# Queries and keys projected together in units of one k block and 1024 columns

## The chip, the cores and the metric

The kernel runs on one core of one Trainium2 chip. The metric is the device time of one execution in microseconds; the time before is the median of three runs. The core's engines are TensorE (PE in the profile, its weight loads PEld), VectorE (DVE), ScalarE (ACT), GpSimd (POOL) and SyncE (SP), which issues most of the transfers.

## The reference

One decoder layer on x of 256 tokens x 1024 features, in float32. A combined projection gives the columns of a retention part and of a block attention part; both outputs are concatenated and go through one output projection, then a SwiGLU network follows.

```python
h = rmsnorm(x, pre_mix_norm)
proj = h @ w_in                                  # 1024 x 3072
rq, rk, rv, rg, mq, mk, mv = split(proj)         # 256, 256, 512, 512, 512, 512, 512 columns
ret = silu(rg) * head_rmsnorm(retention(rotary(rq), rotary(rk) * 64 ** -0.5, rv))
moba = moba_attention(mq, mk, mv, rel_bias)      # 8 heads of 64, causal softmax in one block of 256
x = x + rmsnorm(concat([ret, moba]) @ w_out, post_mix_norm)
h = rmsnorm(x, pre_ffn_norm)
x = x + rmsnorm((silu(h @ w_gate) * (h @ w_up)) @ w_down, post_ffn_norm)
```

## The kernel before

**Arithmetic.** Each float32 operand of a projection is split into a rounded high part and a rest, both in a format that TensorE takes at one pass. ScalarE makes the high part (`w_hi`, `a_hi`), VectorE the rest (`w_lo`, `a_lo`). A product of a 128x128 tile of x and 128x512 of weights is then three matmuls into one PSUM bank (`product`, L940 to L944): hi by hi, hi by lo, lo by hi. The norm's gain is folded into x; the row factor 1/rms is applied when PSUM is copied out.

**Units.** `w_in` is cut into six groups of 512 columns, in the order attention queries (0), attention keys (1), attention values (2), retention queries and keys (3), retention values (4), retention gate (5). A group is four units; a unit is 128x1024 of weights (512 KB): two k blocks of 128 rows, 512 columns of each. There are 24 units, u = 0 to 23, and TensorE does 12 matmuls in each: 2 token tiles, 2 k blocks, 3 products. Group g accumulates over its four units in the two banks of `pj[g % 2]`, one bank for each token tile: bank01 for even groups, bank23 for odd ones. So the copies out of one group run while TensorE fills the other pair.

**Transfers.** SyncE issues all weights in one queue, in the order of units (L343 to L371). `raw` has six slots: the load of unit n waits for `lo_ready` n - 5. The first four units (HALVED) are loaded in two halves of 512 columns, with the transposed x between them: block 0 alone (with the gains), block 1 alone, then pairs of blocks, one pair per unit. x in natural layout (`xs`, for the row factors) goes out ahead of units 5 and 6. GpSimd issues the relative bias: a small row is computed by TensorE after unit 1 (L1021), copied by ScalarE (`brow`), stored, and read back as a 1 MB tile (L425), for which it also waits until all eight `x_lo` are there.

**ScalarE and VectorE.** Before the main loop ScalarE goes through units 0 to 3 (L472 to L486): half of the weights, one block of x, the other half, the next block; then `hi_in(4)`. In step u of the main loop it does `hi_in(u + 5)` (LEAD), which waits for the transfer and for a free slot of the ring of eight, and around it what the attention needs. The placement is by hand: the brow copy in step 0, squares of x in steps 0 and 1 (L527), the query copies `rows_out(qn, ...)` in step 4 after `hi_in(9)`, their transposed copies in step Q_T + 1 = 7 (L517), the key copies in step 8 after `hi_in(13)`, their transposed copies in step K_T + 1 = 10. VectorE mirrors this with `lo_in`.

**TensorE.** In units 0 to 3 `first_unit` (L962) waits for each half by itself. From unit 4 on one wait for `lo_ready` covers the unit. Before a group reuses a pair of banks, TensorE waits for the copies out of them: group 2 for `q_nat` (L996), group 3 for `k_nat`. After unit 6 it transposes the queries (L1023), after unit 9 the keys (L1029), each in eight 128x128 transposes, and from unit 10 on it does the scores of one head after each unit.

`wait_projection` (L303) tells who copies when a group's tile is complete: tile 0 by `proj_done`, tile 1 by `w_used` after the fourth unit of the group.

Of the kernel before, what the change touches and what calls it, by code (L numbers as in the profile page):

```python
# [15 lines left out]
P = 128  # L34
D = 1024
S = 256
# [16 lines left out]
UPG = NK * CW // UNIT  # L53
KPU = UNIT // CW
N_IN = NG * UPG
WOUT_K = [4, 5, 6, 7, 0, 1, 2, 3]
# [17 lines left out]

Q_T, K_T, S0, RQK_T = 6, 9, 10, 18
PT_LAG, PV_LAG = 2, 3
# [12 lines left out]
def hybrid_layer(nc, xt, x, g_post_mix, g_pre_ffn, g_post_ffn, rel_bias,  # L89
                 w_in, w_out, w_gu, w_dn, ident_c, rope_c, decay_c, bucket_c, bias_row, out):  # L90
    with ExitStack() as ctx:
# [101 lines left out]
        d_used = sem("d_used")  # L193
        xt_loaded = [sem(f"xt_loaded{i}") for i in range(NK // KPU)]
        xt_first = sem("xt_first")
        x_loaded = [sem(f"x_loaded{t}") for t in range(NT)]
# [90 lines left out]
        def wait_x_block(eng, k):  # L287

            if k == 0:
                eng.wait_ge(xt_first, 16)  # L290
            elif k == 1 or k % KPU == 0:
                eng.wait_ge(xt_loaded[k // KPU], 16)

# [9 lines left out]
        def wait_projection(eng, group, t):  # L303
            if t == 0:
                eng.wait_ge(proj_done, group + 1)
            else:
                eng.wait_ge(w_used, UPG * (group + 1))
# [23 lines left out]
        def _(sp):  # L331
# [5 lines left out]

            def load_x(k0, k1, done):

                a, b = (NK + k0 * S if k0 else 0), NK + k1 * S  # L340
                sp.dma_start(xT[:, a:b], xt[:, a:b]).then_inc(done, 16)

            for n in range(N_IN):  # L343
                if 5 <= n < 5 + NT:
                    sp.dma_start(xs[:, n - 5, :], x[(n - 5) * P:(n - 4) * P, :]).then_inc(x_loaded[n - 5], 16)
                if n == 6:
                    sp.dma_start(ident[:, :], ident_c).then_inc(ident_loaded, 16)
                if n < HALVED:

                    for i in range(KPU):  # L350
                        sp.dma_start(raw[:, n, i * CW:(i + 1) * CW], w_in[n][:, i * CW:(i + 1) * CW]
                                     ).then_inc(raw_half[n] if i == 0 else raw_loaded[n], 16)
                        if n == 0:
# [96 lines left out]
        def _(act):  # L450
# [20 lines left out]
            act.activation(warm[:, :], half[:, :], ACT.Copy).then_inc(warmed, 1)  # L471
            for i in range(NK // KPU):  # L472
                for k in range(KPU * i, KPU * (i + 1)):
                    if i < HALVED:

                        cols = slice(k % KPU * CW, (k % KPU + 1) * CW)
                        if k % KPU == 0:
                            act.wait_ge(raw_half[i], 16)
                        else:
                            wait_raw(act, i)  # L480
                        act.activation(w_hi[:, i, cols], raw[:, i, cols], ACT.Copy
                                       ).then_inc(hi_half if k % KPU == 0 else hi_ready, 1)
                    wait_x_block(act, k)
                    act.activation(a_hi[:, k, :], x_block(k), ACT.Copy, scale=gain(k)).then_inc(x_hi, 1)
                if i >= HALVED:
                    hi_in(i)  # L486
            hi_in(4)

# [18 lines left out]
            for u in range(N_IN):  # L507
# [152 lines left out]
        def _(dve):  # L660
# [21 lines left out]

            for i in range(NK // KPU):
                for k in range(KPU * i, KPU * (i + 1)):
                    if i < HALVED:
                        cols = slice(k % KPU * CW, (k % KPU + 1) * CW)
                        dve.wait_ge(hi_half if k % KPU == 0 else hi_ready, i + 1)
                        dve.tensor_tensor(w_lo[:, i, cols], raw[:, i, cols], w_hi[:, i, cols].bitcast(F32),
                                          ALU.subtract).then_inc(lo_half if k % KPU == 0 else lo_ready, 1)
                    wait_x_block(dve, k)  # L690
                    dve.wait_ge(x_hi, k + 1)
                    dve.scalar_tensor_tensor(out=a_lo[:, k, :], in0=x_block(k), scalar=gain(k),
                                             in1=a_hi[:, k, :].bitcast(F32), op0=ALU.mult,
                                             op1=ALU.subtract).then_inc(x_lo, 1)
                if i >= HALVED:
                    lo_in(i)
            lo_in(4)

# [33 lines left out]
            for u in range(N_IN):  # L732
# [15 lines left out]
                if u <= S0 + PT_LAG + MH:  # L748
                    for n in LO_UNITS.get(u, [u + LEAD]):
                        lo_in(n)  # L750
                if u < NT:
                    factor(X_, u, 2 * u + 2)
# [186 lines left out]
        def _(pe):  # L939
# [22 lines left out]
            def first_unit(u):  # L962

                for i in range(KPU):
                    k, cols = KPU * u + i, slice(i * CW, (i + 1) * CW)
                    pe.wait_ge(hi_half if i == 0 else hi_ready, u + 1)
                    pe.wait_ge(x_hi, k + 1)
                    for t in range(NT):
                        pe.matmul(pj[0][:, t, :], a_hi[:, k, tile(t)], w_hi[:, u, cols],  # L969
                                  start=(k == 0), stop=False)  # L970
                    pe.wait_ge(lo_half if i == 0 else lo_ready, u + 1)
                    for t in range(NT):
                        pe.matmul(pj[0][:, t, :], a_hi[:, k, tile(t)], w_lo[:, u, cols],  # L973
                                  start=False, stop=False)
                    pe.wait_ge(x_lo, k + 1)
                    for t in range(NT):
                        ins = pe.matmul(pj[0][:, t, :], a_lo[:, k, tile(t)], w_hi[:, u, cols],  # L977
                                        start=False, stop=(k == NK - 1))
                        if t == 0 and k == NK - 1:
                            ins.then_inc(proj_done, 1)  # L980
# [5 lines left out]
            for u in range(N_IN):  # L986
# [3 lines left out]
                else:  # L990
                    pe.wait_ge(lo_ready, u + 1)
                for t in range(0 if u < HALVED else NT):
                    if s == 0:
# [9 lines left out]
                    for i in range(KPU):  # L1003
                        k = KPU * s + i
                        if g == 0 and t == 0:
                            pe.wait_ge(x_lo, k + 1)
                        ins = product(pj[g % 2][:, t, :], a_hi[:, k, tile(t)], a_lo[:, k, tile(t)],
# [3 lines left out]
                    if s == UPG - 1 and t == 0:  # L1011
                        ins.then_inc(proj_done, 1)
                if u >= HALVED:
                    ins.then_inc(w_used, 1)
# [227 lines left out]
def _laid_out(i):  # L1242

    def a(name):
        return np.asarray(i[name])

    x = a("x")[0]
    w_in = a("w_in")[0].reshape(UPG, KPU, P, NG, CW)[:, :, :, ORDER]
    gate = a("w_gate")[0].reshape(GU, KPU, P, NF, FG)
# [8 lines left out]
        "rel_bias": a("rel_bias"),  # L1258
        "w_in": w_in.transpose(3, 0, 2, 1, 4).reshape(N_IN, P, UNIT),
        "w_out": a("w_out")[0].reshape(NK, P, D)[WOUT_K],  # L1260
# [18 lines left out]
```

## Time and profile before

| | us |
|---|---|
| median of 3 runs | 318.85 |
| lowest and highest run | 318.06, 322.44 |
| span of the profiled execution | 316.7 |
| TensorE busy in it | 307.7 (97%) |
| VectorE busy | 180.9 (57%) |
| ScalarE busy | 150.9 (48%) |
| GpSimd busy | 24.6 (8%) |

The profile is of one execution; its span is what the engines' records cover, and the times of the runs hold a little around it too. Busy times of different engines overlap and do not add up. Matmuls are pipelined: the record of one is longer than the distance to the next.

### The profile page before, as it was taken

To read this page: it belongs to the slowest core of one execution; us is meant where nothing else is said; L and a number is where in the kernel's file an instruction comes from. 1 tells how busy PE (TensorE), PEld (TensorE's weight loads), DVE (VectorE), ACT (ScalarE), POOL (GpSimd) and SP (SyncE) were. 2 spreads that over 40 slices of the span, in tenths; PEclk is the share of its full clock that TensorE was granted. 3 is DMA by queue.
4 is the path that set the end of the run, shared out by engine and by line. 5 is a ranking of instruction groups with operands and counts; after the bars stand their busy time and mean duration, and the time that the engine had idled before them with its cause. 6 is when DMAs were issued, how large, how long until landed. Compare 5 with 4: busy or idle time off the path is not lost.

```text
span 316.7 us, 4110 instructions
## 1 busy us (share of the span) xinstructions
PE 307.7 (97%) x1432; PEld 247.1 (78%) x1432; DVE 180.9 (57%) x255; ACT 150.9 (48%) x248; POOL 24.6 (8%) x27
## 2 busy tenths in 40 slices
PE   6999999999999999999999999999999999999992
PEld 3788867778888888778888888888888888888881
DVE  2858447675467497899555555544444454551426
ACT  5887654436409164676444444444433333340322
POOL 2020045000002000540000000000000000000001
PEclk9999999999999999999999999999999999999998
DMA  7999994405451553279955555555655655400003
GB/s 212 405 406 378 411 395 138 148 26 184 150 155 46 199 155 112 71 220 314 340 179 174 179 193 185 167 178 191 199 199 199 199 197 192 141 0 0 0 2 132
DMA packets 17518, 58.35 MB, mean 184 GB/s; under 512 B 1998, under 2 KB 2518, under 8 KB 17505
## 3 DMA queue, kind: packets, MB, share of 16 engines
q1 hardware_dynamic: 17136, 57.06, 52.3%
q0 software_dynamic: 368, 1.11, 1.0%
q8 instruction: 8, 0.13, 0.2%
q14 instruction: 6, 0.04, 0.0%
HBM read 57.10 MB, written 1.06 MB: 184 GB/s over the span
## 4 chain that ended last, share of the span: by engine, by line
PE 90%; DVE 4%; POOL 2%; DMA 2%; ACT 1%; issue 0%; SPq 0%; DVEq 0%
PE bank L942 26%; PE bank L944 26%; PE bank L943 25%; PE bank L952 4%; DMA raw<-in_w_in 2%; PE bank L969 1%; POOL xs L442 1%; PE bank L1043 1%; PE bank L1041 1%; PE bank L973 1%; PE bank L977 1%; DVE d_lo L867 1%; DVE res L933 1%; DVE w_lo L860 1%; PE bank L1075 1%; DVE res L927 1%
## 5 line engine op out<-in xcount | busy, mean ns | idle before, releaser
L942 PE MATMUL bank<-w_hi,a_hi 128*128 128x512 f32 x256 | 101.7, 397 | 0.0
L944 PE MATMUL bank<-w_hi,a_lo 128*128 128x512 f32 x256 | 100.1, 391 | 0.0
L943 PE MATMUL bank<-w_lo,a_hi 128*128 128x512 f32 x256 | 99.7, 390 | 0.0
L944 PEld LDWEIGHTS bank<-w_hi,a_lo 128*128 128x128 f32 x256 | 48.0, 188 | 10.5
L942 PEld LDWEIGHTS bank<-w_hi,a_hi 128*128 128x128 f32 x256 | 48.1, 188 | 10.3 <-issue 0.7
L608 ACT ACTIVATE sil<-bank,rstd 128x256 f32<-128x256 f32 x22 | 10.4, 473 | 95.8 <-PE bank L944 93.4
L943 PEld LDWEIGHTS bank<-w_lo,a_hi 128*128 128x128 f32 x256 | 48.1, 188 | 9.8
L860 DVE TENSOR_TENSOR w_lo<-raw,w_hi 128x1024 fp32r<-128x1024 f32 x40 | 49.5, 1276 | 6.5 <-ACT w_hi L593 6.5
L875 DVE SCALAR_TENSOR_TENSOR hid<-bank,rstd,sil 128x256 f32<-128x256 f32 x22 | 10.6, 484 | 74.3 <-ACT sil L608 74.3
L672 DVE TENSOR_TENSOR w_lo<-raw,w_hi 128x1024 fp32r<-128x1024 f32 x32 | 40.3, 1281 | 17.9 <-ACT w_hi L456 17.9
L593 ACT ACTIVATE w_hi<-raw 128x1024 fp32r<-128x1024 f32 x40 | 40.4, 1057 | 0.0
L942 PE MATMUL bank<-d_hi,h_hi 128*128 128x512 f32 x88 | 36.6, 415 | 0.2 <-DVE d_lo L867 0.2
L456 ACT ACTIVATE w_hi<-raw 128x1024 fp32r<-128x1024 f32 x32 | 32.7, 1051 | 6.6 <-DMA raw<-in_w_in 4.3
L944 PE MATMUL bank<-d_hi,h_lo 128*128 128x512 f32 x88 | 34.8, 395 | 0.0
L943 PE MATMUL bank<-d_lo,h_hi 128*128 128x512 f32 x88 | 34.3, 390 | 0.0
L867 DVE TENSOR_TENSOR d_lo<-raw,d_hi 128x1024 fp32r<-128x1024 f32 x22 | 26.0, 1218 | 0.9 <-ACT d_hi L601 0.9
L601 ACT ACTIVATE d_hi<-raw 128x1024 fp32r<-128x1024 f32 x22 | 22.3, 1059 | 0.8 <-DMA raw<-in_w_dn 0.8
L410 POOL TENSOR_TENSOR rstd<-va,half 128x1 f32<-128x1 f32 x8 | 5.3, 669 | 201.7 <-DVE va L678 201.7
L944 PEld LDWEIGHTS bank<-d_hi,h_lo 128*128 128x128 f32 x88 | 16.5, 188 | 3.9
L942 PEld LDWEIGHTS bank<-d_hi,h_hi 128*128 128x128 f32 x88 | 16.5, 188 | 3.4 <-DVE d_lo L867 0.6
L943 PEld LDWEIGHTS bank<-d_lo,h_hi 128*128 128x128 f32 x88 | 16.6, 189 | 2.9
L513 ACT ACTIVATE pr<-pr,lmin 128x128 f32<-128x128 f32 (+1 forms) x16 | 7.2, 448 | 18.7 <-DVE lmin L726 18.7
(116 smaller groups left out, 299.2 us busy)
## 6 DMA issues: line engine op xcount, KB each, us to landing
raw<-in_w_gu SPq DMA_DIRECT2D x44, 512.0 KB, 4.5
raw<-in_w_dn SPq DMA_DIRECT2D x22, 512.0 KB, 4.7
raw<-in_w_in SPq DMA_DIRECT2D x20, 512.0 KB, 9.1
raw<-in_w_out SPq DMA_DIRECT2D x8, 512.0 KB, 3.2
raw<-in_w_in SPq DMA_DIRECT2D x8, 256.0 KB, 5.5
xs<-in_x SPq DMA_DIRECT2D x2, 512.0 KB, 8.2
bias<-bias_row POOLq DMA_DIRECT2D x1, 1024.0 KB, 9.8
out<-res SPq DMA_DIRECT2D x4, 256.0 KB, 2.0
```

The lines of the kernel that those rows point to most:

```text
L456: act.activation(w_hi[:, n % RING, :], raw[:, n % RAW, :], ACT.Copy).then_inc(hi_ready, 1)
L593: act.activation(w_hi[:, a0 % RING, :], raw[:, n0 % RAW, :], ACT.Copy).then_inc(hi_ready, 1)
L601: act.activation(d_hi[:, (DN * g0 + j) % DRING, :], raw[:, n0 % RAW, :], ACT.Copy).then_inc(hi_ready, 1)
L608: act.activation(sil[:, t, :], pg[:, t, 0:FG], ACT.Silu, scale=rstd[:, X1_, t:t + 1]).then_inc(sil_ready[t], 1)
L672: dve.tensor_tensor(w_lo[:, n % RING, :], raw[:, n % RAW, :], w_hi[:, n % RING, :].bitcast(F32), ALU.subtract).then_inc(lo_ready, 1)
L860: dve.tensor_tensor(w_lo[:, slot, :], raw[:, n0 % RAW, :], w_hi[:, slot, :].bitcast(F32), ALU.subtract).then_inc(lo_ready, 1)
L867: dve.tensor_tensor(d_lo[:, slot, :], raw[:, n0 % RAW, :], d_hi[:, slot, :].bitcast(F32), ALU.subtract).then_inc(lo_ready, 1)
L875: dve.scalar_tensor_tensor(out=hid[:, t, :], in0=pg[:, t, FG:2 * FG], scalar=rstd[:, X1_, t:t + 1], in1=sil[:, t, :], op0=ALU.mult, op1=AL ...
L942: pe.matmul(acc, hi, wh, start=first, stop=False)
L943: pe.matmul(acc, hi, wl, start=False, stop=False)
L944: return pe.matmul(acc, lo, wh, start=False, stop=last)
L952: ins = pe.transpose(dst[:, b * P:(b + 1) * P], src[:, b * P:(b + 1) * P], ident[:, :])
```

## The change

Groups 0 and 1 (queries and keys) are taken together as eight units (QK = 8) of one k block and 1024 columns: the left half of a unit is queries, the right half keys. All four banks, `pj[0]` and `pj[1]`, are filled over units 0 to 7. The bytes of a unit, the matmuls of a unit and their number in all stay as they are; groups 2 to 5 are unchanged. With this:

- x is loaded in eight single blocks, block n + 1 behind the weights of unit n; ScalarE and VectorE round block k + 1 behind unit k: blocks 0 to 5 ahead of the main loop, 6 and 7 in its steps 0 and 1, after `hi_in(5)` and `hi_in(6)`.
- `first_unit` uses the same block of x for both halves and writes them to different pairs of banks; a new `both_unit` does units 4 to 7, in the order queries tile 0, queries tile 1, keys tile 0, keys tile 1.
- The query copies move from step 4 of ScalarE's loop to step 7, after `hi_in(12)`; the key copies from step 8 to step 7, right behind them and ahead of `hi_in(13)`.
- The query transposes move from unit 6 to unit 8 (Q_T), their copies from step 7 to step 9. The keys' stay.
- `wait_projection` counts anew, and the host lays `w_in` out accordingly.

```diff
-Q_T, K_T, S0, RQK_T = 6, 9, 10, 18
+Q_T, K_T, S0, RQK_T = 8, 9, 10, 18
...
         def wait_projection(eng, group, t):
-            if t == 0:
-                eng.wait_ge(proj_done, group + 1)
+
+            if (group, t) == (0, 1):
+                eng.wait_ge(proj_done, 2)
+            elif t == 0:
+                eng.wait_ge(proj_done, group + 1 + min(group, 1))
+            elif group == 1:
+                eng.wait_ge(w_used, QK)
             else:
                 eng.wait_ge(w_used, UPG * (group + 1))
...
                     for i in range(KPU):
                         sp.dma_start(raw[:, n, i * CW:(i + 1) * CW], w_in[n][:, i * CW:(i + 1) * CW]
                                      ).then_inc(raw_half[n] if i == 0 else raw_loaded[n], 16)
-                        if n == 0:
-                            load_x(i, i + 1, xt_first if i == 0 else xt_loaded[0])
-                        elif i == 0:
-                            load_x(KPU * n, KPU * (n + 1), xt_loaded[n])
-                elif n < NK // KPU:
-                    load_x(KPU * n, KPU * (n + 1), xt_loaded[n])
+                        if n == 0 and i == 0:
+                            load_x(0)
+                    load_x(n + 1)
+                elif n < NK:
                     load(n, n % RAW, w_in[n])
+                    if n + 1 < NK:
+                        load_x(n + 1)
...
+            for k in range(LEAD):
+                if k < HALVED:
+                    act.wait_ge(raw_half[k], 16)
+                    act.activation(w_hi[:, k, 0:CW], raw[:, k, 0:CW], ACT.Copy).then_inc(hi_half, 1)
+                    if k == 0:
+                        x_hi_part(0)
+                    wait_raw(act, k)
+                    act.activation(w_hi[:, k, CW:UNIT], raw[:, k, CW:UNIT], ACT.Copy).then_inc(hi_ready, 1)
+                else:
+                    hi_in(k)
+                x_hi_part(k + 1)
...
                 hi_in(u + LEAD)
+                if u + LEAD + 1 < NK:
+                    x_hi_part(u + LEAD + 1)
...
-                if u == UPG:
+                if u == QK - 1:
                     act.wait_ge(nq_ready, 1)
                     wait_factor(act, X_, NT - 1)
                     rows_out(qn, 0, lambda t: nq[:, t:t + 1], q_nat)
-                if u == 2 * UPG:
                     rows_out(kn, 1, r_x, k_nat)
...
+            def both_unit(u):
+
+                pe.wait_ge(x_lo, u + 1)
+                for i in range(KPU):
+                    for t in range(NT):
+                        ins = product(pj[i][:, t, :], a_hi[:, u, tile(t)], a_lo[:, u, tile(t)],
+                                      w_hi[:, u, i * CW:(i + 1) * CW], w_lo[:, u, i * CW:(i + 1) * CW],
+                                      first=False, last=(u == QK - 1))
+                        if u == QK - 1 and (i, t) != (KPU - 1, NT - 1):
                             ins.then_inc(proj_done, 1)
                 ins.then_inc(w_used, 1)
```

## Rows read from the trace of the kernel before

**Rows 1.** The page's first part: busy time, share of the span, instructions

```profile
span 316.7 us, 4110 instructions
PE 307.7 (97%) x1432; PEld 247.1 (78%) x1432; DVE 180.9 (57%) x255; ACT 150.9 (48%) x248; POOL 24.6 (8%) x27
```

**Rows 2.** Busy time of each engine in four stretches; last: clock, DMA share, GB/s

```profile
0.00:20.00 20.00, 17.61 (x68) 11.76 (x69) 11.35 (x20) 13.86 (x26) 2.20 (x10) 1.00 0.91 328
20.00:40.00 20.00, 20.00 (x98) 16.28 (x96) 12.35 (x12) 15.14 (x22) 2.07 (x3) 1.00 1.03 396
40.00:60.00 20.00, 20.00 (x97) 15.07 (x97) 11.11 (x28) 10.83 (x27) 8.08 (x3) 1.00 0.65 245
120.00:140.00 20.00, 19.19 (x94) 15.65 (x93) 16.10 (x21) 11.66 (x23) 8.59 (x7) 1.00 0.35 108
```

**Rows 3.** The chain of waits in order of time: start, length, what

```profile
7.13 0.41 ACT a_hi L484
7.67 0.70 PE bank L969 x2
...
26.58 0.87 PE bank L952 x8
...
35.66 0.87 PE bank L952 x8
```

**Rows 4.** Timeline of the first units: start, length, engine, instruction, idle before it

```profile
1.19 0.43 SPq L341 DMA_DIRECT2D xT<-in_xt  x1
4.63 0.51 ACT L484 ACTIVATE a_hi<-xT 128x256 fp32r<-128x256 f32 x1 [0.16 <-DMA xT<-in_xt]
5.28 0.70 PE L969 MATMUL bank<-w_hi,a_hi 128*128 128x512 f32 x2 [0.41 <-ACT a_hi L484]
5.82 0.62 PE L973 MATMUL bank<-w_lo,a_hi 128*128 128x512 f32 x2
6.28 0.61 PE L977 MATMUL bank<-w_hi,a_lo 128*128 128x512 f32 x2
6.50 0.63 ACT L481 ACTIVATE w_hi<-raw 128x512 fp32r<-128x512 f32 x1 [1.36 <-DMA raw<-in_w_in]
7.03 0.49 ACT L484 ACTIVATE a_hi<-xT 128x256 fp32r<-128x256 f32 x1
7.16 0.69 DVE L688 TENSOR_TENSOR w_lo<-raw,w_hi 128x512 fp32r<-128x512 f32 x1 [1.42 <-ACT w_hi L481]
7.47 0.63 ACT L481 ACTIVATE w_hi<-raw 128x512 fp32r<-128x512 f32 x1
7.67 0.70 PE L969 MATMUL bank<-w_hi,a_hi 128*128 128x512 f32 x2 [0.78 <-ACT a_hi L484]
9.12 0.61 PE L969 MATMUL bank<-w_hi,a_hi 128*128 128x512 f32 x2
```

**Rows 5.** Timeline of ScalarE and VectorE around the query copies

```profile
16.86 1.06 ACT L456 ACTIVATE w_hi<-raw 128x1024 fp32r<-128x1024 f32 x1 [1.51 <-DMA raw<-in_w_in]
19.63 1.06 ACT L456 ACTIVATE w_hi<-raw 128x1024 fp32r<-128x1024 f32 x1
20.72 1.23 DVE L672 TENSOR_TENSOR w_lo<-raw,w_hi 128x1024 fp32r<-128x1024 f32 x1 [0.82 <-ACT w_hi L456]
21.96 2.94 ACT L456 ACTIVATE w_hi<-raw 128x1024 fp32r<-128x1024 f32 x3
24.81 1.24 ACT L493 ACTIVATE qn<-bank,nq 128x512 f32<-128x512 f32 x2
27.16 1.06 ACT L456 ACTIVATE w_hi<-raw 128x1024 fp32r<-128x1024 f32 x1 [0.16 <-DMA raw<-in_w_in]
28.12 1.07 ACT L500 ACTIVATE qT<-bank 128x512 f32<-128x512 f32 x2
32.58 1.06 ACT L456 ACTIVATE w_hi<-raw 128x1024 fp32r<-128x1024 f32 x1 [2.44 <-DMA raw<-in_w_in]
```

**Rows 6.** Issues of units 11, 12 and 13, each with its time to landing

```profile
L336 SPq DMA_DIRECT2D raw<-in_w_in x1: 328/328/328, 19.2 to 19.2; - x1
DMA to landing us min/median/max: 7.9/7.9/7.9
...
L336 SPq DMA_DIRECT2D raw<-in_w_in x1: 328/328/328, 22.0 to 22.0; - x1
DMA to landing us min/median/max: 6.5/6.5/6.5
...
L336 SPq DMA_DIRECT2D raw<-in_w_in x1: 327/327/327, 24.3 to 24.3; - x1
DMA to landing us min/median/max: 8.3/8.3/8.3
```

**Rows 7.** Timeline of GpSimd: the bias row stored, the bias tile loaded

```profile
18.57 0.51 POOL L420 DMA_DIRECT2D bias_row<-brow  x1 [15.97 <-ACT brow L523]
23.53 0.96 POOL L425 DMA_DIRECT2D bias<-bias_row  x1 [0.59 <-DMA bias_row<-brow]
```

More of the change, by code:

```diff
@@ L54 @@
 KPU = UNIT // CW
+QK = KPU * UPG
 N_IN = NG * UPG
@@ L193, in hybrid_layer @@
         d_used = sem("d_used")
-        xt_loaded = [sem(f"xt_loaded{i}") for i in range(NK // KPU)]
-        xt_first = sem("xt_first")
+        xt_loaded = [sem(f"xt_loaded{k}") for k in range(NK)]
         x_loaded = [sem(f"x_loaded{t}") for t in range(NT)]
@@ L287, in wait_x_block @@
         def wait_x_block(eng, k):
[L289 to L292, printed above, removed]
+            eng.wait_ge(xt_loaded[k], 16)
         def wait_raw(eng, n, rounds=0):
@@ L336, in load, with load_x @@
                 sp.dma_start(raw[:, slot, :], src).then_inc(raw_loaded[slot], 16)
-            def load_x(k0, k1, done):
-                a, b = (NK + k0 * S if k0 else 0), NK + k1 * S
-                sp.dma_start(xT[:, a:b], xt[:, a:b]).then_inc(done, 16)
+            def load_x(k):
+                a, b = (NK + k * S if k else 0), NK + (k + 1) * S
+                sp.dma_start(xT[:, a:b], xt[:, a:b]).then_inc(xt_loaded[k], 16)
             for n in range(N_IN):
@@ L471, in _, with x_hi_part @@
             act.activation(warm[:, :], half[:, :], ACT.Copy).then_inc(warmed, 1)
[L472 to L487, printed above, removed]
+            def x_hi_part(k):
+                wait_x_block(act, k)
+                act.activation(a_hi[:, k, :], x_block(k), ACT.Copy, scale=gain(k)).then_inc(x_hi, 1)
+            for k in range(LEAD):
[9 more added lines that the diff above has]
+                x_hi_part(k + 1)
             def rows_out(dst, group, scale, done):
@@ L681, in _, with x_lo_part @@
             dve.memset(junk[:, 0:CW // 2], 0.0).then_inc(zeros_ready, 1)
[L683 to L697, printed above, removed]
+            def x_lo_part(k):
+                wait_x_block(dve, k)
+                dve.wait_ge(x_hi, k + 1)
+                dve.scalar_tensor_tensor(out=a_lo[:, k, :], in0=x_block(k), scalar=gain(k),
+                                         in1=a_hi[:, k, :].bitcast(F32), op0=ALU.mult,
+                                         op1=ALU.subtract).then_inc(x_lo, 1)
+            for k in range(LEAD):
+                if k < HALVED:
+                    for cols, ready, done in ((slice(0, CW), hi_half, lo_half),
+                                              (slice(CW, UNIT), hi_ready, lo_ready)):
+                        dve.wait_ge(ready, k + 1)
+                        dve.tensor_tensor(w_lo[:, k, cols], raw[:, k, cols], w_hi[:, k, cols].bitcast(F32),
+                                          ALU.subtract).then_inc(done, 1)
+                        if k == 0 and done is lo_half:
+                            x_lo_part(0)
+                else:
+                    lo_in(k)
+                x_lo_part(k + 1)
             def rotary(t):
@@ L750, in _ @@
                         lo_in(n)
+                if u + LEAD + 1 < NK:
+                    x_lo_part(u + LEAD + 1)
                 if u < NT:
@@ L964, in first_unit @@
                 for i in range(KPU):
-                    k, cols = KPU * u + i, slice(i * CW, (i + 1) * CW)
+                    cols = slice(i * CW, (i + 1) * CW)
                     pe.wait_ge(hi_half if i == 0 else hi_ready, u + 1)
-                    pe.wait_ge(x_hi, k + 1)
+                    pe.wait_ge(x_hi, u + 1)
                     for t in range(NT):
-                        pe.matmul(pj[0][:, t, :], a_hi[:, k, tile(t)], w_hi[:, u, cols],
-                                  start=(k == 0), stop=False)
+                        pe.matmul(pj[i][:, t, :], a_hi[:, u, tile(t)], w_hi[:, u, cols],
+                                  start=(u == 0), stop=False)
                     pe.wait_ge(lo_half if i == 0 else lo_ready, u + 1)
                     for t in range(NT):
-                        pe.matmul(pj[0][:, t, :], a_hi[:, k, tile(t)], w_lo[:, u, cols],
+                        pe.matmul(pj[i][:, t, :], a_hi[:, u, tile(t)], w_lo[:, u, cols],
                                   start=False, stop=False)
-                    pe.wait_ge(x_lo, k + 1)
+                    pe.wait_ge(x_lo, u + 1)
                     for t in range(NT):
-                        ins = pe.matmul(pj[0][:, t, :], a_lo[:, k, tile(t)], w_hi[:, u, cols],
-                                        start=False, stop=(k == NK - 1))
-                        if t == 0 and k == NK - 1:
+                        ins = pe.matmul(pj[i][:, t, :], a_lo[:, u, tile(t)], w_hi[:, u, cols],
+                                        start=False, stop=False)
+                ins.then_inc(w_used, 1)
+            def both_unit(u):
+                pe.wait_ge(x_lo, u + 1)
+                for i in range(KPU):
[4 more added lines that the diff above has]
+                        if u == QK - 1 and (i, t) != (KPU - 1, NT - 1):
                             ins.then_inc(proj_done, 1)
@@ L991, in _ @@
                     pe.wait_ge(lo_ready, u + 1)
-                for t in range(0 if u < HALVED else NT):
+                    if u < QK:
+                        both_unit(u)
+                for t in range(0 if u < QK else NT):
                     if s == 0:
@@ L1004, in _ @@
                         k = KPU * s + i
-                        if g == 0 and t == 0:
-                            pe.wait_ge(x_lo, k + 1)
                         ins = product(pj[g % 2][:, t, :], a_hi[:, k, tile(t)], a_lo[:, k, tile(t)],
@@ L1012, in _ @@
                         ins.then_inc(proj_done, 1)
-                if u >= HALVED:
+                if u >= QK:
                     ins.then_inc(w_used, 1)
@@ L1247, in _laid_out @@
     x = a("x")[0]
-    w_in = a("w_in")[0].reshape(UPG, KPU, P, NG, CW)[:, :, :, ORDER]
+    w_in = a("w_in")[0].reshape(NK, P, NG, CW)
+    both = w_in[:, :, ORDER[:KPU]].reshape(QK, P, UNIT)
+    w_in = w_in.reshape(UPG, KPU, P, NG, CW)[:, :, :, ORDER[KPU:]]
     gate = a("w_gate")[0].reshape(GU, KPU, P, NF, FG)
@@ L1258, in _laid_out @@
         "rel_bias": a("rel_bias"),
-        "w_in": w_in.transpose(3, 0, 2, 1, 4).reshape(N_IN, P, UNIT),
+        "w_in": np.concatenate([both, w_in.transpose(3, 0, 2, 1, 4).reshape(N_IN - QK, P, UNIT)]),
         "w_out": a("w_out")[0].reshape(NK, P, D)[WOUT_K],
```

## The prediction

> **What bounds the kernel now.** I read five views, from coarse to fine. The page's first part [rows 1] says that TensorE is the bound: busy 97% of a span of 316.7 us, with every other engine below 60%. The table of stretches [rows 2] says that in the part the diff touches there is nothing left to win in the middle: from 20 to 60 us TensorE is busy 20.00 of every 20.00 us at a granted clock of 1.00. Only the first stretch has idle time (17.61 of 20.00 us busy). The same table shows what stands right behind TensorE: the DMA engines have a share of 0.91 and then 1.03, so until 40 us the weights arrive as fast as they ever will. Everything that ScalarE does "as soon as its weights land" is therefore timed by the memory.
>
> The chain of waits [rows 3] gives the TensorE clockwork that I need below. Its pieces from 7.67 us on are TensorE alone, each starting where the last one ends. Unit 7 starts at 26.58 + 0.87 = 27.45, the key turn after unit 9 starts at 35.66, so three units take 8.21 us and one takes 2.74 us. The query turn costs 0.87 us, the key turn too.
>
> The timeline of the first 13 us [rows 4] shows the only wait that the change can shorten. TensorE finishes the first half of unit 0 at 6.89, and then sits 0.78 us until 7.67. Two things had to come: the second half of the weights (landed at 6.50, rounded by ScalarE until 7.13) and the second block of x, which ScalarE can only round after that (7.03 to 7.52). The last one decides.
>
> **Part 1: one block of x per unit.** The second half of unit 0 now uses the same block of x as the first, so the wait for the second a_hi is gone. What is late next? The rounded weights are ready at 7.13; a release took 0.14 us in the first half (a_hi ends at 5.14, the matmul starts at 5.28), so the first pair starts at about 7.27 and takes 0.54 us. But its next pair needs w_lo, which VectorE writes from 7.16 to 7.85 [rows 4], so it starts at about 7.98 instead of 7.67 + 0.54 = 8.21. Gain: **0.24 us**. After this the trace has no TensorE wait for x or weights that could be shortened: unit 1 starts right behind at 9.12, and what it needs was rounded from 7.47 on [rows 4]. With x spread over eight units the same bytes are needed later, which adds slack, not time: w4 to w6 come up to 384 KB earlier in the queue.
>
> The queue is the same to within an order: the whole x (1 MB) and the weights up to unit 7 are in it before w8, as now. So w8 to w12 should land when they land now. Nor are the pieces too many for SyncE: it issues thirteen transfers before w4 in both kernels, and by w12 it issues 6.5 us ahead of the landing [rows 6], against three extra issues of 0.43 us [rows 4]. A price for the 1 KB rows of the smaller x pieces is not in the trace; bounds are 0 and these three issues, 1.3 us; I take 0, since the engines have a backlog to work on.
>
> **Part 2: four banks, and both projections end at once.** TensorE issues the same matmuls: 12 a unit, the same stationary tiles, 0.23 us apart. The query turn moves from unit 6 to unit 8 and the key turn stays at 9: two turns of 0.87 us, before and after. No cost.
>
> What moves is the time at which the query banks must be free. Before, qn is evicted by ScalarE at 24.81 (two of 0.62 us) [rows 5], while TensorE fills the other pair of banks with keys until 30.19; nobody waits. After, units 0 to 7 fill all four banks, and unit 8 (values) wants bank01 back at the very moment unit 7 ends. When is that? Before, unit 7 starts at 27.45; without the query turn ahead of it (0.87) and with the 0.24 us gained it starts at 26.34 and ends at **29.08**.
>
> When is q_nat there? The order of loops in the new unit helps: query tiles are finished first, so the first is complete three matmuls into unit 7, at about 27.0. ScalarE, however, reaches its copies behind hi_in(12) in the same step of its loop. That instruction waits for w12. The DMA answer [rows 6] has w12 issued at 22.0 and landing 6.5 us later, at **28.5**; w11 at 19.2 + 7.9 = 27.1 agrees with the row where ScalarE waited for it at 27.16 [rows 5]. Before, w12's wait is invisible, since ScalarE spent 28.12 to 29.1 on qT. Now it is the front of a queue: hi_in(12) from 28.5, the next ScalarE instruction 0.95 us behind (three hi_in start from 21.96 on, and the next instruction starts at 24.81), thus qn tile 0 from 29.45 to 30.1, and TensorE goes on at about 30.25. Stall: 30.25 - 29.08 = 1.17 us. The second query tile is ready at 30.7, and TensorE needs it only 1.37 us after the first. I take **1.2 us**.
>
> Is w12's issue later? It waits for lo_ready 7, the w_lo of unit 6, which ends at 21.95 [rows 5]. New in front of its hi_in (19.63) is one rounding of x, 0.5 us on ScalarE; but that stretch begins when w5 lands (16.86, after a wait of 1.51 us), and w5 now has 256 KB less ahead of it, 0.65 us at 396 GB/s [rows 2, 5]. The two cancel, and this w_lo stays where it is within some 0.2 us. The Trainium skill's page "DMA: Bandwidth & Descriptors", section "Queues, rings and completion order", says that descriptors are consumed in ring order on each engine and that engines take turns between queues; by that the landing of w12 hangs on the bytes before it, as I assume, and on the bias load of the other queue, which is the second rival. The trace agrees as far as the landings of w11 and w12 lie 1.4 us apart.
>
> **Behind the stall.** ScalarE now evicts four tiles in a row: to 30.7 for the queries, to about 31.9 for the keys, and then hi_in(13), whose weights land at 24.3 + 8.3 = 32.6 [rows 6]: no loss there. qT follows the query turn (which ends near 33.9) at 33.5 to 35, kT the key turn near 37.4; the first scores come after unit 10, with kT over 1 us ahead. k_nat is first needed by unit 12 and the key turn, both far. POOL's bias load waits for x_lo of block 7, now at about 22.5, but it went out at 23.53 behind brow_stored anyway [rows 7], and brow stays at its place. So the rest of the kernel is moved as a whole: its later gaps (19.19 of 20.00 us busy between 120 and 140 [rows 2]) hang on chains that start from TensorE's own work.
>
> **Sum.** -0.24 + 1.2 = +1.0 us. The profiled execution goes from 316.7 to 317.7 us; the median of the runs (318.85) lies 2.15 us above that span, as it must contain what is around it, so the time goes to **319.9 us**.
>
> **Rivals.**
>
> No stall (chance 0.17). If w12 lands 1.2 us earlier, or ScalarE's copies come in time, only the 0.24 us remain: 318.6 us. For it: w12's landing is that of one execution, and another may have a faster memory. Against it: w12 must beat 27.4, and even w11 lands at 27.1.
>
> A longer stall (0.17). The bias load (1 MB, issued on POOL's queue at 23.53 [rows 7]) competes with w12. In this trace w12 still lands 1.4 us behind w11, but w13, behind the small rope table, lands 4.1 us after w12, ScalarE waiting 2.44 us for it [rows 5]. If w12 is caught as w13 was, it lands up to 2.7 us later, and as the path runs through it, all of that counts: +3.7 us, 322.6 us. The 1.3 us bound of the x pieces would act at the same place: 321.2.
>
> TensorE's clock (0.03), the case on the other side. The units 0 to 7 now cycle through four banks, and a gap of 1.2 us is cut in behind them. If the granted clock fell from its upper level (2.4 GHz) to 1.2 GHz, each unit would cost 2.74 us more; it decides (over 6.4 us) from 2.3 units on, and over eight units it gives 340.8 us. Against it: the rows from 40 to 60 us, where between the units small matmuls go to other banks and still 1.00 is granted, and the 0.8 us idle between 120 and 140, also at 1.00 [rows 2]. The Trainium skill's page "TensorE: Matmul & The Clock Gate", section "A second HAM failure mode: psum-queue depth-cycling", reports a kernel that cycled through PSUM banks and whose clock went up and down for it; the trace so far speaks against that.
>
> **How the numbers follow.** The forecast has 0.58: the stall between 0.5 and 2 us, 319.1 to 320.7. Then 0.17, 0.17 and 0.03 for the rivals, and 0.05 for something not seen, either way. The range reaches down past the case without a stall, to 318.1 us (the lowest run was 318.06), and up to where most of the longer stalls lie, 322.0; that leaves out under 2 in 10. Two per cent (6.4 us) is about what a measurement of this kernel can tell from no change; nearly all the cases are within it: faster 0.02, same 0.94, slower 0.04.
>
> **What would show it.** Right: a single new TensorE gap of about 1.2 us between 29 and 30.3 us, released by the first qn copy of ScalarE; hi_in(12) starting when w12 lands and qn right behind; the gap at 7.67 shrunk by 0.24 us; everything after unit 8 at the old distance plus 1.0 us. Wrong: w12 landing before 27.5 (no gap), a TensorE wait for weights in units 4 to 7 (then the roundings of x in the first two steps are too dear), a granted clock below 1.00 there, or the loss given back in a later gap.

## The result and the profile after

The changed kernel is slower: 321.73 us median (20 runs, 319.34 to 324.36) against 318.69 us (318.06 to 322.44, but 19 of 20 runs at or below 319.13). The ratio is 1.0091, with a 95% interval of 1.0074 to 1.0108, that is +2.9 us. Not only the median moved: the runs of the changed kernel spread over 5 us where all but one of those before lie within 1.1 us. Whatever the cause is, it differs from run to run.

The mean granted clock of each of the 20 executions is on record too, and it parts them in two. Ten have 0.986 to 0.992 and take 322.08 to 324.36 us, 323.0 on average; the other ten have 0.994 to 0.998 and take 319.34 to 321.38 us, 320.4 on average. The profiled one, with 0.992, belongs to the first ten. Of 54 executions of the kernel before, timed beside the experiments, 53 have 0.994 to 0.999 and one has 0.986 (324.04 us).

The profiled execution has a span of 320.3 us, 3.6 more than before. Busy time of each engine in the stretches of [rows 2], and in two short ones, of the changed kernel (columns as there; the last three are granted clock, DMA share, GB/s):

```profile
0.00:20.00 20.00, 18.39 (x70) 12.01 (x71) 10.97 (x19) 13.92 (x25) 2.67 (x10) 1.00 0.88 321
20.00:40.00 20.00, 17.84 (x81) 14.48 (x80) 11.53 (x12) 13.60 (x21) 1.59 (x3) 0.91 1.03 400
40.00:60.00 20.00, 20.00 (x94) 14.59 (x92) 10.22 (x23) 10.68 (x25) 8.15 (x3) 1.00 0.59 224
120.00:140.00 20.00, 19.19 (x94) 15.64 (x93) 16.52 (x25) 10.09 (x21) 7.73 (x7) 1.00 0.37 129
...
31.00:33.00 2.00, 1.90 (x6) 1.54 (x7) 0.64 (x1) 1.69 (x3) 0.00 (x0) 0.65 1.03 397
33.00:35.00 2.00, 2.00 (x6) 1.58 (x5) 0.59 (x1) 1.06 (x1) 0.00 (x0) 0.50 1.03 421
```

The second row has lost 2.16 us of TensorE's busy time, all in one place, and its mean clock is 0.91. The short rows show where: behind the gap, from about 31.6 to 35.0 us, TensorE had 0.50 of its clock, the lower of its two levels. The timeline of the changed kernel around the gap (start, length, engine, instruction, idle before it and its releaser):

```profile
28.55 0.39 PE L933 MATMUL bank<-w_hi,a_lo 128*128 128x512 f32 x1
29.32 1.06 ACT L439 ACTIVATE w_hi<-raw 128x1024 fp32r<-128x1024 f32 x1 [0.86 <-DMA raw<-in_w_in]
30.29 1.25 ACT L475 ACTIVATE qn<-bank,nq 128x512 f32<-128x512 f32 x2
31.10 0.47 PE L931 MATMUL bank<-w_hi,a_hi 128*128 128x512 f32 x1 [2.16 <-ACT qn L475]
31.42 1.26 ACT L475 ACTIVATE kn<-bank,rstd 128x512 f32<-128x512 f32 x2
33.32 1.06 ACT L439 ACTIVATE w_hi<-raw 128x1024 fp32r<-128x1024 f32 x1 [0.63 <-DMA raw<-in_w_in]
...
33.36 0.63 PE L931 MATMUL bank<-w_hi,a_hi 128*128 128x512 f32 x1
33.78 0.63 PE L932 MATMUL bank<-w_lo,a_hi 128*128 128x512 f32 x1
34.21 0.63 PE L933 MATMUL bank<-w_hi,a_lo 128*128 128x512 f32 x1
...
35.51 1.04 PE L941 MATMUL bank<-ident,qn 128*128 128x128 f32 x8
```

This is the chain of the forecast, link by link: ScalarE waits 0.86 us for w12, rounds it, then copies the first query tile, and that releases TensorE. It is 2.16 us long and not 1.2. And unit 8 then takes 4.41 us (31.10 to 35.51) instead of 2.74: eight of its matmuls stand 0.43 us apart, where at the upper level they stand 0.23 us apart. Gap and lower clock are 3.8 us; the start was 0.36 us earlier (unit 1 begins at 8.76, in [rows 4] at 9.12).

So the profile alone invites the story "a longer gap, and the clock". It fits the ten executions with a lower clock at best. The ten others lie 1.7 us above the kernel before, and the experiments show that more than the gap takes part.

### The profile page after: what moved, and what is told of

Its sections match the earlier page's. It is cut to its first block, busy times and chain, and to the rows that moved or that the text cites. A ratio compares the mean times of both kernels' runs of the same rounds, so it can differ in the third digit from the quotient of the medians.

```text
span 320.3 us, 4120 instructions
## 1 busy us (share of the span) xinstructions
PE 309.9 (97%) x1432; PEld 248.1 (77%) x1432; DVE 181.1 (57%) x255; ACT 151.1 (47%) x248; POOL 24.7 (8%) x27
## 4 chain that ended last, share of the span: by engine, by line
PE 83%; DMA 5%; DVE 4%; SPq 2%; ACT 2%; POOL 2%; issue 1%; DVEq 0%; ACTq 0%
PE bank L931 25%; PE bank L933 24%; PE bank L932 24%; DMA raw<-in_w_in 5%; PE bank L941 4%; POOL xs L425 1%; PE bank L1042 1%; SPq L334 1%; PE bank L1040 1%; SPq L324 1%; DVE d_lo L856 1%; ACT junk L448 1%; DVE res L922 1%; DVE w_lo L849 1%; PE bank L1074 1%
```

## Experiments

All ratios are to the kernel before on the same chip, with 95% intervals. They are not ratios of the medians given below. The experiments ran on three chips: e1 to e4 on one, e5 to e8 on another, e9 and e10 on a third. The changed kernel itself was not timed again beside e5, nor e3 beside e6, so these pairs are compared by way of the kernel before.

| kernel | ratio | interval |
|---|---|---|
| changed, query copies first (e1) | 0.9999 | 0.999 to 1.0008 |
| changed, bias load late (e2) | 1.0113 | 1.0093 to 1.0132 |
| before, gap 1.3 us (e3) | 1.0077 | 1.0061 to 1.0092 |
| before, gap 1.7 us (e4) | 1.0099 | 1.0066 to 1.0132 |
| changed, GpSimd products late (e5) | 1.0037 | 1.0023 to 1.0051 |
| e3 with GpSimd products late (e6) | 1.0039 | 1.0024 to 1.0055 |
| before, GpSimd products late (e7) | 1.0002 | 0.9993 to 1.0011 |
| e10 with GpSimd products late (e8) | 1.0018 | 1.0005 to 1.003 |
| before, longest gap, products late (e9) | 1.0168 | 1.0154 to 1.0181 |
| e1 with key copies back in step 8 (e10) | 1.0004 | 0.9994 to 1.0015 |

### The query copies ahead of the rounding of w12

```diff
+                if u == QK - 1:
+                    act.wait_ge(nq_ready, 1)
+                    wait_factor(act, X_, NT - 1)
+                    rows_out(qn, 0, lambda t: nq[:, t:t + 1], q_nat)
                 hi_in(u + LEAD)
...
                 if u == QK - 1:
-                    act.wait_ge(nq_ready, 1)
-                    wait_factor(act, X_, NT - 1)
-                    rows_out(qn, 0, lambda t: nq[:, t:t + 1], q_nat)
                     rows_out(kn, 1, r_x, k_nat)
```

> The changed kernel with one thing moved: in step 7 of ScalarE's loop the two query copies stand before hi_in(12) instead of behind it. My theory (the extra time of the changed kernel is the TensorE gap ahead of unit 8, 2.16 us, plus the half clock of about eight matmuls that follows it, some 1.6 us, both from the query copies standing behind the wait for w12): no gap between units 7 and 8, a granted clock of 1.00 from 20 to 40 us, and a time 0.2 to 0.5 us below the kernel before, ratio 0.998 to 0.9995; the runs lie as close together as those of the kernel before. Rival (four banks or the finer pieces of x cost something of their own, in unit after unit or in the clock): the gap goes but the clock still falls or the units are longer, and the ratio stays above 1.003.

Measured: 318.73 us against 318.77, ratio 0.9999, and the 11 runs lie between 318.44 and 319.45. One moved block of ScalarE's program takes away the whole loss and the scatter with it. Busy time by stretch in this kernel:

```profile
20.00:28.00 8.00, 8.00 (x37) 6.64 (x36) 6.31 (x9) 7.35 (x11) 2.08 (x3) 1.00 1.03 396
28.00:31.00 3.00, 3.00 (x15) 2.48 (x14) 2.13 (x3) 3.00 (x6) 0.00 (x0) 1.00 0.99 365
31.00:33.00 2.00, 2.00 (x14) 1.76 (x13) 0.65 (x1) 1.47 (x2) 0.00 (x0) 1.00 1.03 404
```

TensorE has no idle time there and the full clock, with the same four banks and the same pieces of x. That excludes, down to about 0.3 us (the interval), the rival that these cost something by themselves. All 11 executions have a granted clock of 0.994 to 0.999. What it doesn't give is the expected gain of 0.2 to 0.5 us: see the part on the prediction.

### What delays w12?

The landing of w12 was 0.8 us later than in [rows 6], and the bias load had gone out 0.44 us earlier. So I held the bias load back:

```diff
             pool.wait_ge(x_lo, NK)
+            pool.wait_ge(lo_ready, 13)
```

> The changed kernel, but GpSimd issues the 1 MB bias load only when the low part of unit 12 is written, so that it cannot share the DMA engines with w12. Theory A (w12 landed 0.8 us later than before because the bias load went out 0.44 us earlier and takes turns with it): w12 lands at 27.9 to 28.4, the gap ahead of unit 8 shrinks from 2.16 to 0.7 to 1.2 us, and, if a gap of that size leaves the clock alone, the time is 2.5 to 3 us below the changed kernel, ratio to before about 1.002 to 1.004. Rival B (the smaller pieces of x make the queue slower): w12 still lands at 29 or later, gap and time stay as in the changed kernel. The bias tile must be there at about 43 us; landing by then needs under 12 us and should just do; if it is late, the first scores show the wait.

Measured: 322.86 us, ratio 1.0113: not faster, and by the intervals not told apart from the changed kernel (1.0091). w12 landed at 28.6 and the gap ahead of unit 8 shrank to 1.0 us, as theory A had it. But the bias landed only at 42.8 and VectorE waited 1.9 us for it, and further on there was a TensorE wait of 1.6 us that neither theory had. So the time decides nothing on theory A. The other profiles do, against it and against rival B too: the landing of w12, read like [rows 6], was 28.6 with the query copies first, 28.0 in the later run of the changed kernel (e5), 28.1 to 28.4 in four kernels with the transfers of before (e3, e4, e6, e7), but 29.2 in a fifth (e9), where neither the bias load nor x had been touched. It scatters by over a microsecond, from a cause that no run shows. The late landing of the profiled execution needs no cause in the change.

### A gap of its own, without the change

To see what a gap costs, I cut one into the kernel before. TensorE waits ahead of unit 8 for something that comes a little later:

```diff
                 else:
                     pe.wait_ge(lo_ready, u + 1)
+                if u == 8:
+                    pe.wait_ge(lo_ready, 13)      # e3, and in e6
```

> The kernel before, with TensorE made to wait ahead of unit 8 until the low part of unit 12 is written: a gap of about 1.2 us cut into otherwise unchanged work with two banks at a time. Theory (the clock falls because of the idle time, not because of the banks, and a gap of 1.2 us is too short for it mostly): +1.2 us, ratio 1.003 to 1.005, clock 1.00. If short gaps suffice: +2.8 us, ratio about 1.009. Rival (only four banks bring the clock down): +1.2 us and clock 1.00 here, and also in the run with the longer gap.

In e4 the added wait is `pe.wait_ge(raw_loaded[13 % RAW], 16 * (13 // RAW + 1))`.

> The kernel before, with TensorE made to wait ahead of unit 8 until the weights of unit 13 have landed: a gap of about 2.4 us, a little longer than in the changed kernel, with two banks at a time. Theory (idle time brings the clock down): the gap plus a stretch at a granted clock of 0.5 behind it in some executions or all, +2.4 us alone or up to +4.2 us with it, ratio 1.0075 to 1.013, and runs that scatter more than those of the kernel before. Rival (the banks do it): +2.4 us in every run, clock 1.00, ratio 1.0075.

Measured: medians of 321.35 us (ratio 1.0077) and 321.29 us (1.0099), four runs each. By the medians both cost about 2.5 us, whatever the gap, and e3 costs twice what was expected. The ratio of e4 is the higher one because of one run of 323.54 us, which has a granted clock of 0.992; the seven others of the two kernels have 0.995 to 0.998. So in these seven it is not the clock. Who waited for whom on TensorE in e3 (total, times, longest):

```profile
PE bank L1043 <- DVE lmin L726: 1.6, 1, 1.6
PE bank L942 <- DVE w_lo L672: 1.3, 1, 1.3
```

The gap I made is 1.3 us; in e4 it was 1.7 us, where 2.4 had been expected. But a second wait of 1.6 us (1.0 in e4) has come: TensorE waits some 20 us later for the minimum of a head's scores (`lmin`). The chain of waits of e3 tells why (start, length, what):

```profile
45.03 3.21 DVE w_lo L672
48.24 0.20 DVE pr L726
...
49.14 0.68 ACT pr L513 x3
49.82 0.96 ACT w_hi L456
50.78 0.02 issue
50.80 3.23 DVE w_lo L672
54.03 0.20 DVE pr L726
...
54.64 0.49 PE bank L1043 x2
```

Two w_lo of VectorE (L672) take 3.2 us each; all the others of this line take at most 1.23. They stand ahead of the head's scores in VectorE's order, so the minimum comes late, ScalarE's exponentials and next rounding come late after it, and that w_lo later still. The timeline of e3 shows what lies beside them:

```profile
44.79 5.69 POOL L431 TENSOR_TENSOR xg<-xs,gp 128x1024 f32<-128x1024 f32 x2 [19.52 <-issue]
45.03 3.21 DVE L672 TENSOR_TENSOR w_lo<-raw,w_hi 128x1024 fp32r<-128x1024 f32 x1 [2.00 <-ACT w_hi L456]
50.56 2.40 POOL L433 TENSOR_TENSOR gp<-gm,gp 128x1024 f32<-128x1024 f32 x1
50.80 3.23 DVE L672 TENSOR_TENSOR w_lo<-raw,w_hi 128x1024 fp32r<-128x1024 f32 x1 [2.00 <-ACT w_hi L456]
```

Each begins 0.24 us after a GpSimd product of two SBUF tiles, and lasts 2.0 us longer than alone, about the 2.16 us that were left of the 2.40 us product. In the kernel before there is one such (timeline):

```profile
42.93 1.23 DVE L672 TENSOR_TENSOR w_lo<-raw,w_hi 128x1024 fp32r<-128x1024 f32 x1 [2.00 <-ACT w_hi L456]
43.93 4.83 POOL L431 TENSOR_TENSOR xg<-xs,gp 128x1024 f32<-128x1024 f32 x2 [19.45 <-issue]
46.71 3.13 DVE L672 TENSOR_TENSOR w_lo<-raw,w_hi 128x1024 fp32r<-128x1024 f32 x1 [2.00 <-ACT w_hi L456]
48.84 3.25 POOL L433 TENSOR_TENSOR gp<-gm,gp 128x1024 f32<-128x1024 f32 x1
52.40 1.23 DVE L672 TENSOR_TENSOR w_lo<-raw,w_hi 128x1024 fp32r<-128x1024 f32 x1 [1.53 <-ACT w_hi L456]
```

The w_lo at 42.93 begins before the products and the third one at 52.40 after them; the one in the middle loses 1.9 us, and no TensorE wait follows. The product behind it takes 3.25 instead of 2.40 us, so each delays the other. The Trainium skill, "SBUF — State Buffer", section "SBUF: two separate sides", states that VectorE, with two SBUF inputs, and GpSimd hold a shared pair of ports exclusively for a whole instruction, and the other blocks. By that rule a w_lo loses what is left of the product, here 2.16 us; the traces nearly agree, with 2.0 us.

What matters is who sets the start of each. The products begin when gains arrive by transfer, at 43.9 to 44.8 in all these kernels: the transfers set their time (in the kernel before the last gain lands at 43.8). TensorE sets that of the w_lo of a head. Anything that shifts TensorE alone slides one set over the other.

### Taking the collision away

GpSimd's products are needed much later, by the output norm. I held them back until all heads are done:

```diff
             pool.wait_ge(gp_loaded, 16)
+            pool.wait_ge(pv_done, MH)
```

Once in the changed kernel:

> The changed kernel, with GpSimd's three 128x1024 products (xg and gp, from about 44 us on) held back until the attention's eight heads are done (about 80 us). Theory C (three costs, the last one seen only in the gap kernels so far: a w_lo of VectorE that falls under a GpSimd product takes 3.2 instead of 1.23 us, and after a shift of 1 to 3 us it is the one ahead of the next head's minimum, so TensorE waits 1.0 to 1.6 us more): no w_lo over 1.3 us between 40 and 60 us, no TensorE wait on the minimum, and a median 0.5 to 1.5 us below the changed kernel, ratio to before 1.005 to 1.008; what is left is the gap ahead of unit 8 and, in some runs, the half clock. Rival (the collision does not take part in the changed kernel, whose profiled run shows none on the path): ratio stays at 1.009.

Once in the two-bank kernel with the cut gap, and once in the kernel before as the control:

> The kernel before with the gap of about 1.3 us ahead of unit 8 (TensorE waits for the low part of unit 12) and with GpSimd's products held back. Theory C: only the gap itself is left, +1.2 to +1.4 us, ratio 1.0035 to 1.005, against 1.0077 with the products in their place. Rival (a gap costs more by the clock, in runs that were not profiled): ratio stays above 1.006 and the runs scatter.

> The control: the kernel before with GpSimd's products held back until the heads are done. Its slow w_lo (3.13 us at 46.7) is off the path of TensorE, so every theory expects no change, ratio 0.999 to 1.001. If the products, now at 80 to 90 us, hit something tight there, the ratio is above 1.002, and e5 and e6 have to be read against this one.

Measured: the control stays at 1.0002. The changed kernel falls from 1.0091 to 1.0037 (319.81 us), below the 1.005 to 1.008 that I expected, and its six runs lie within 1.3 us (319.25 to 320.49) instead of 5. The two-bank kernel with the gap falls from 1.0077 to 1.0039, as expected. Between 40 and 60 us neither has a slow w_lo left, and none has a TensorE wait for the minimum. In e5 the change has these two waits on TensorE, of which the first, in unit 0, stands in the place of the 0.78 us of [rows 4]:

```profile
PE bank L959 <- ACT w_hi L467: 0.7, 1, 0.7
PE bank L932 <- ACT qn L476: 0.5, 1, 0.5
```

For the two-bank kernel this settles it: the profile of e3 shows the collision and the second wait, that of e6 shows neither, the gap is about the same (1.3 and 1.1 us), and no run of either has a lower clock. The collision costs it some 1.2 us.

For the changed kernel the ratio speaks against the rival, that the collision takes no part: with GpSimd's products held back 1.7 of the 2.9 us are gone. How they go is less clear. None of the six runs of e5 has a lower clock (0.995 to 0.998), where ten of twenty had. Without these ten the changed kernel would lie 1.7 us above the kernel before and not 2.9, so its runs at the full clock lie only some 0.5 us above e5. That much is the collision's part if the low clock is left out. And the profiled execution of the changed kernel shows no second wait. Its gap and its low clock had shifted TensorE by 3.64 us (first scores at 42.85 against 39.21), nearly the 3.80 us between two heads, and the pattern was back in step, with one slow w_lo:

```profile
50.14 2.38 POOL L416 TENSOR_TENSOR gp<-gm,gp 128x1024 f32<-128x1024 f32 x1
50.35 3.25 DVE L655 TENSOR_TENSOR w_lo<-raw,w_hi 128x1024 fp32r<-128x1024 f32 x1 [2.00 <-ACT w_hi L439]
```

Its half clock at 31 us came before any product had begun, so their absence can't have removed that one. Either the clock fell later in the other executions, behind a second wait as in e2 (below), or the six runs of e5 were spared by luck: if every second run had it, six in a row without it would come once in 64. No run decides this. Nor is 1.2 us the cost of e5's own gap: the gap was 0.5 us in the profiled execution, which was the fastest of the six.

### What brings the clock down?

> The kernel before (two banks at a time) with GpSimd's products held back, and TensorE made to wait ahead of unit 8 until the high part of unit 13 is written: a gap of about 3.4 us. The half clock has been seen in two profiled runs only, behind gaps of 2.16 and 1.6 us, and not behind others of 1.0 to 1.7 us. Theory (a long enough gap alone brings it, and the longer the more often): a granted clock of 0.50 for some 3 us behind the gap in the profile, +3.4 us and in most runs 1.5 us more, ratio 1.013 to 1.017. Rival (it takes the four banks, or something else of the changed kernel): clock 1.00 throughout and the gap alone, ratio 1.0095 to 1.011.

The edit is `pe.wait_ge(hi_ready, 14)` in the place of the wait in e6. Measured: 323.85 us, 1.0168. The profile shows a gap of 4.6 us instead of 3.4, since w13 landed at about 33.7 and not at 32.6 as in [rows 6], and after it:

```profile
31.00:34.00 3.00, 0.00 (x0) 0.00 (x0) 0.71 (x1) 0.29 (x1) 0.00 (x0) 0.99 1.02 395
34.00:36.00 2.00, 1.13 (x3) 0.97 (x4) 1.20 (x1) 2.00 (x4) 0.00 (x0) 0.50 1.01 415
36.00:38.00 2.00, 2.00 (x7) 1.52 (x6) 1.13 (x2) 0.87 (x1) 0.00 (x0) 0.50 1.04 422
38.00:40.00 2.00, 2.00 (x6) 1.61 (x5) 0.13 (x1) 0.00 (x0) 0.00 (x0) 0.50 1.01 406
40.00:44.00 4.00, 4.00 (x22) 3.28 (x21) 0.00 (x0) 0.18 (x1) 0.00 (x0) 0.91 1.03 410
```

The clock fell at the end of the gap, at about 33.9 us, and was back at about 40.7. With two banks at a time, TensorE ran at half clock for some 6 us of work. So the gap is enough to bring it about; the four banks are not needed. All six runs of e9 have a mean clock of 0.984 to 0.992, none of the 11 of e7, which lacks only the gap. In e2 it came after a wait of 1.6 us, the one for the minimum:

```profile
54.00:56.00 2.00, 1.90 (x11) 1.57 (x12) 0.52 (x3) 1.92 (x5) 0.00 (x0) 0.83 0.63 227
56.00:58.00 2.00, 2.00 (x8) 1.71 (x8) 1.95 (x6) 0.15 (x2) 0.00 (x0) 0.50 0.13 47
```

and did not come after a wait of just that length in e3. Over these profiles: gaps up to 1.3 us never, 1.6 to 1.7 us once in three, 2.16 and 4.6 us both times. The mean clocks of the timed runs tell how often it came. The three profiled executions with such a stretch have 0.989 to 0.992, the eight without it 0.995 to 0.999, and no run of any kernel lies between 0.992 and 0.994. It is 0.992 or less in 10 of 20 runs of the changed kernel, 3 of 5 of e2, none of 4 of e3, 1 of 4 of e4, none of e5, e6, e7, e8, e10 and e1, and all 6 of e9. Where in those executions it came, and behind which wait, only the profiled ones show.

### Versions meant to keep the gain

> A version meant to keep what the change gives: the changed kernel with the query copies ahead of hi_in(12), the key copies back in step 8 behind hi_in(13), and GpSimd's products held back. Theory: no gap, clock 1.00, and the 0.2 us of the earlier second half of unit 0; ratio 0.998 to 1.000. If one block of x per unit gives nothing in the end, exactly 1.000.

> The version with the query copies ahead of hi_in(12) and the key copies back in step 8 behind hi_in(13), with GpSimd's products where they were. It tells whether the 0.2% by which the earlier version with both moves lay above the kernel before came from the key copies or from the held back products. If from the products: ratio 0.999 to 1.0005, as for the query copies alone (0.9999). If from the key copies: 1.001 to 1.003.

Measured: 319.29 us (1.0018) and 318.68 us (1.0004, not told apart from 1). e8 misses its expectation of 0.998 to 1.000. The ratio of e10 is the one expected if the held back products add the small loss of e8. But the two intervals overlap (1.0005 to 1.003, 0.9994 to 1.0015), the two ran on different chips, in the control the held back products cost nothing, and the profiled execution of e8 (span 316.9) shows no wait to explain a loss. So this stays open. No version beats the kernel before. The best use of the change is e1, which is level with it.

## Why the prediction was right and where it was wrong

The direction, the mechanism and the order of size were right: a loss well within two per cent, inside the range of 318.1 to 322.0, by a stall between units 7 and 8. The time itself was 1.8 us too low (319.9 against 321.73), above the 319.1 to 320.7 that I had given the likeliest case: a loss of 1.0 us forecast, 2.9 measured. That the median lies inside the range is in part luck. The room above 320.7 was meant for a w12 caught by the bias load or slowed by the smaller pieces of x, and neither happened; the ten runs with the lower clock all lie above 322.0.

**The gain at the start.** Forecast 0.24 us. From the landing of the second half of unit 0 to the first matmul of unit 1 it was 2.62 us before (6.50 to 9.12, [rows 4]), 2.45 us in the changed kernel (6.31 to 8.76) and 2.44 us in e1 (6.73 to 9.17): 0.17 to 0.18 us. The step was right, but it is smaller than the scatter of the landing itself (6.31 to 6.73), and no median shows it.

**The stall.** The step "query copies behind hi_in(12), which waits for w12" was right, as e1 shows by removing it. Its size can be read from single executions only: 0.5 us in e5, 1.0 in e2, 2.16 in the changed kernel, around the forecast 1.2. The spread follows the landing of w12, which scatters from 28.0 (e5) to 29.3. With GpSimd's products away the whole change costs 1.2 us (e5), where the sum had +1.0.

**The step that failed** is the sentence "so the rest of the kernel is moved as a whole". I had followed only chains that start from TensorE. GpSimd's products start from a transfer and stay where they are, and VectorE's w_lo, moved by one to three microseconds, runs into them: twice in e2 (where the late bias had a part in the shift), e3 and e4, with a TensorE wait of 1.0 to 1.6 us behind it, and once in the profiled execution of the changed kernel, without one. The 1.7 us between the changed kernel (2.9) and e5 (1.2) are what the sum lacked. As said above, how they divide between the second wait and the clock is open. I had asked where a stall goes, but not what in the next 20 us keeps its own time. Two rows of the kernel before would have told, and both had been in front of me: GpSimd's busy tenths around 44 us, and the maximum of w_lo, 3131 ns, beside a median of 1225.

**The clock.** I had given it 0.03 and priced it as eight units, for 340.8 us. It came in ten of twenty runs, for a short stretch: eight matmuls after the gap in the profiled one, +1.7 us, and 2.6 us between the averages of the two halves. So the sum had put at nothing a term that adds 1.3 us to the average. The case was drawn at the wrong size and with too small a chance: a short stretch after a gap, not a state that lasts over eight units. The page of the Trainium skill that I set beside it, "TensorE: Matmul & The Clock Gate", "A second HAM failure mode: psum-queue depth-cycling", reports short idle times between groups of matmuls in a kernel that cycles through banks. In this kernel the idle time is what counts and not the banks: e1 has four banks, no gap and a clock of 1.00, e9 two banks, a gap and a clock of 0.50.

**The rivals.** The longer stall was there in the profiled run (2.16), but not for its stated reason: e2 and the landings of the other kernels show no need for the bias load. The case without a stall did not come, though e5 with a gap of 0.5 us came near it.

## What to carry to other kernels

When an in-order engine both feeds the bound engine and frees its banks, put the freeing first: a copy that is ready must not stand behind a wait for memory. Before you say that a small shift moves the rest as a whole, look for work on other engines that is released by transfers, and check whether it shares ports with what moves. And when the runs of a kernel scatter more than they did, one profiled execution shows one of several courses. Sort the timed runs by their mean granted clock first; then take the parts of the loss from timed kernels that lack them one at a time.

## What the runs showed of the hardware

- A VectorE op on two SBUF tiles (128x1024, float32) that begins 0.24 us after a GpSimd product of the same size took 3.2 instead of 1.23 us (e3).
- After an idle gap TensorE's granted clock fell from 1.00 to 0.50 (2.4 to 1.2 GHz): after 2.16 us (changed kernel, for 3.4 us), after 4.6 us (e9, for 6.8 us), and after 1.6 us in e2 (for 3.4 us), but not after 1.6 us in e3, nor after 1.7 us in e4.
- Of the profiled executions of the changed kernel and of e1 to e10, the two with 3.4 us at 0.50 have a mean granted clock of 0.992 and 0.990 over the whole execution, the one with 6.8 us has 0.989, and the eight without such a stretch have 0.995 to 0.999.
- A 512 KB transfer in a full queue (w12), at the same place in the order, landed anywhere from 28.0 to 29.3 us in the profiled executions of these kernels.
